# Output projection as 32 column-block tiles, started while the last scan group drains

## The reference, cut to what matters

```python
hx = modulate(rms_norm(x, g0), mx[0], mx[1]);  hc = modulate(rms_norm(ctx, g0), mc[0], mc[1])
z, xs, B, C, dt = split(silu_conv(h @ w_in))          # w_in: 2048 x 10368
y  = D_skip * xs + sum over two directions of ssd_scan(xs, dt, a, B, C, state from ctx)
yx = rms_norm(y * silu(z), norm_g) @ w_out            # w_out: 4096 x 2048
x  = x + mx[2] * yx
h2 = modulate(rms_norm(x, g1), mx[3], mx[4])
out = x + mx[5] * moe(h2)                             # 32 experts, top-1 group, top-2 experts
```

## Time and profile before

| | |
|---|---|
| median of 3 runs | 2303.89 us (2303.46 to 2305.78) |
| the profiled execution | 2307.22 us |
| its span | 2305.7 us |
| PE / PEld / DVE / ACT / POOL busy | 88 / 53 / 44 / 21 / 5 % of the span |
| last projection of the groups ends | about 1020.9 us |
| last matmul of the output projection ends | about 1260.4 us |
| first transposes of h2 | 1282.9 us |
| HBM traffic | 660 MB, mean 286 GB/s |

### The profile page before, as it was taken

One profiled execution on the slowest core, in us unless ns is written; L12 is line 12 of the kernel. 1 busy time (PEld: TensorE's weight loads), 2 busy tenths in 40 slices (PEclk: granted clock), 3 DMA queues, 4 the chain that ended last, 5 costly groups with the idle time before them and its releaser, 6 DMA issues. The chain is left out here.

```text
span 2305.7 us, 28693 instructions
## 1 busy us (share of the span) xinstructions
PE 2033.7 (88%) x10596; PEld 1219.1 (53%) x10596; DVE 1011.0 (44%) x1619; ACT 487.5 (21%) x519; POOL 108.2 (5%) x148
## 2 busy tenths in 40 slices
PE   4789999999999999975998489888888888888888
PEld 2368777777777777754787343333333333323332
DVE  2264656565655555654555632222222222222223
ACT  3132333333424243422443200000000000000000
POOL 0000000000000000002900000000000000000000
PEclk8689999999999999987999599999999999999999
DMA  7967575666665656563555269999999999999997
GB/s 292 380 198 216 179 210 175 198 186 186 186 198 174 205 168 205 178 203 120 221 197 192 100 248 422 422 422 422 422 422 422 422 422 422 422 422 422 422 422 310
DMA packets 296347, 660.37 MB, mean 286 GB/s; under 512 B 15936, under 2 KB 186304, under 8 KB 241904
## 3 DMA queue, kind: packets, MB, share of 16 engines
q1 hardware_dynamic: 288672, 635.27, 74.4%
q0 software_dynamic: 6672, 24.29, 2.8%
q10 hardware_dynamic: 960, 0.23, 0.0%
HBM read 653.28 MB, written 6.46 MB: 286 GB/s over the span
## 5 line engine op out<-in xcount | busy, mean ns | idle before, releaser
L1614 PE MATMUL bank<-wt,xe 128*64 128x512 f32 x2048 | 466.3, 597 | 111.5 <-DMA wt<-in_moe_w_up 108.4
L1395 PE MATMUL bank<-hTh,whi 128*128 128x256 f32 (+1 forms) x1280 | 414.2, 344 | 0.0
L1396 PE MATMUL bank<-hTl,whi 128*128 128x256 f32 (+1 forms) x1280 | 406.1, 337 | 0.0
L1290 DVE TENSOR_TENSOR x<-x,bank 128x512 f32<-128x512 f32 x256 | 158.3, 680 | 544.6 <-PE bank L1601 544.6
L1614 PEld LDWEIGHTS bank<-wt,xe 128*64 128x64 f32 x2048 | 158.3, 137 | 413.6 <-issue 410.2
L1395 PEld LDWEIGHTS bank<-hTh,whi 128*128 128x128 f32 x1280 | 243.8, 190 | 80.2 <-issue 47.5
L1396 PEld LDWEIGHTS bank<-hTl,whi 128*128 128x128 f32 x1280 | 244.1, 191 | 24.1
L893 DVE TENSOR_TENSOR wlo<-raw,whi 128x2048 fp32r<-128x2048 f32 x80 | 183.2, 2290 | 130.8 <-ACT whi L665 130.4
L1400 PE MATMUL bank<-hTh,wlo 128*128 128x256 f32 (+1 forms) x1280 | 234.9, 336 | 0.0
L1639 PE MATMUL bank<-wt,hdn 128*64 128x512 f32 x1024 | 226.8, 595 | 1.4 <-DVE hdn L1302 1.4
L1400 PEld LDWEIGHTS bank<-hTh,wlo 128*128 128x128 f32 x1280 | 199.8, 190 | 24.9
(11 more groups left out here) (286 smaller groups left out, 1814.8 us busy)
## 6 DMA issues: line engine op xcount, KB each, us to landing
wt<-in_moe_w_gate SPq DMA_DIRECT2D x128, 1024.0 KB, 23.4
wt<-in_moe_w_up SPq DMA_DIRECT2D x128, 1024.0 KB, 25.5
wt<-in_moe_w_down SPq DMA_DIRECT2D x128, 1024.0 KB, 22.4
raw<-in_ssm_w_in SPq DMA_DIRECT2D x80, 1024.0 KB, 6.1
raw<-in_ada_w SPq DMA_DIRECT2D x79, 1024.0 KB, 5.2
raw<-in_ssm_w_out SPq DMA_DIRECT2D x32, 1024.0 KB, 4.8
fr<-in_ada_w SPq DMA_DIRECT2D x17, 1024.0 KB, 14.0
bc<-cum_d POOLq DMA_DIRECT2D x32, 512.0 KB, 7.1
```

The source lines that it names most:

```text
L1290: dve.tensor_tensor(x1[:, tt, cols], x1[:, tt, cols], banks[(1, 3, 6, 7)[nb]][:, :], ALU.add).then_inc(s_acc2, 1)
L1395: pe.matmul(bank[:, 0:width], wh[:, k, :], hTh[:, k, 0:width], start=(k == 0), stop=False)
L1396: last = pe.matmul(bank[:, 0:width], wh[:, k, :], hTl[:, k, 0:width], start=False, stop=False)
L1614: last = pe.matmul(banks[0][SLOTS * h:SLOTS * h + SLOTS, :], xe[:, k, :], wt[2 * q + h][:, FF * i:FF * i + FF], start=(k == 0), stop=(k == ...
```

## The change

1. **First stage.** Nine slots instead of seven; only the last two wait for the transposes. The four `fr` slots at 16, 24, 48 and 56 KB lie over the halves of `hTh` and `hTl` that are filled last. B's tile of `w_in` is loaded right behind the dt tile. PE does blocks 0 to 3, then four times: one block, a quarter of dt, a quarter of projection B (`b_part`). C and x0 are projected before `dt_turn`, which writes banks 4 and 5; DVE's and ACT's dt work is mixed with the work for B, C and x0.
2. **Scan output.** `finish` gets two more DVE operations: a copy of y to fp32r and the difference. POOL stores both (`yh_d`, `yl_d`; twice the bytes). They are loaded straight to `yh` and `yl`; `norm_g` goes to `w_out`'s rows instead.
3. **Output projection.** 32 tiles of 512 rows by 512 columns (`OTILES`), seven of column block 0, seven of block 1, the last group's two, then blocks 2 and 3. ACT and DVE work on each in four pieces with `norm_g` as scale. The first ten tiles stand in the drain's ten steps. A column block leaves PSUM two tiles after it is done; the squares' reduction comes two tiles before the end.
4. tanh of B and x chunks is written in place by ACT; the MoE's last two weight buffers, `x1`, `h2` and others lie elsewhere.

```diff
-    FSLOT = [0, 1, 2, 3, 4] * 2 + [5, 6, 0, 1, 2, 3, 4] * 3 + [5, 6]
+    FSLOT = [0, 1, 2, 3, 4, 5, 6] * 2 + [7, 8, 3, 4, 5, 6, 7, 8, 3, 4, 5, 6, 7, 8, 4, 6, 7, 8, 4]
+    OTILES = [(nb, q) for nb in range(2) for q in range(GROUPS - 1)] + [(0, GROUPS - 1), (1, GROUPS - 1)]
+    OTILES += [(nb, q) for nb in range(2, 4) for q in range(GROUPS)]
...
# SP
+                if pos == DT_POS:
+                    front_free(max(q for q in range(FRONT) if FSLOT[q] == 0))
+                    sp.dma_start(w_view(raw, 0), w_in[:, :, bass.ds(w_in_at(0, 0), P)]).then_inc(s_raw[0], 16)
...
+            for i, (nb, q) in enumerate(OTILES):
...
+                    sp.wait_ge(s_lo, M_OUT + i - RAW + 1)
+                sp.dma_start(a_view(raw_of(OUT0 + i)), w_out[:, 4 * q:4 * q + 4, 512 * nb:512 * nb + 512])
+                if i == RAW - 1:
+                    sp.wait_ge(s_win, M_OUT)
+                    for g in range(GROUPS - 1):
+                        y_load(g)
+                if i == OLAST[0] - 1:
+                    y_load(GROUPS - 1)
+                    sp.dma_start(x1[:, :, :], t["x"][0]...)
+                    sp.dma_start(rw...)   ...
# POOL, per k of 32
+                pool.tensor_tensor(yk, yh[:, k, :], yl[:, k, :], ALU.add)
                 pool.tensor_tensor(yk, yk, yk, ALU.mult)
                 pool.tensor_tensor(ysq[:, 1, :], ysq[:, 1, :], ysq[:, 0, :], ALU.add)
# ACT
+            def out_hi(i):
+                act.wait_ge(s_raw[raw_of(OUT0 + i)], ...)
+                act.wait_ge(s_wh, m - 1)
+                act.wait_ge(s_lo, m - 1)
+                for j in range(4):
+                    last = act.activation(whi[:, m % 2, 512 * j:512 * j + 512], raw[...], ACT.Copy, scale=ngcol[:, 4 * q + j:4 * q + j + 1])
...
+                    if not w:
+                        out_hi(n + 1)
                     if ssd and n in (0, 4):
                         decays(s, n // 4)
# DVE
                 dve.tensor_tensor(ybuf[:, c % 2, :], ybuf[:, c % 2, :], zs[:, c, :], ALU.mult).then_inc(s_fin2, 1)
+                dve.wait_ge(s_fin2, GC * s + (c + 1))
+                dve.tensor_copy(yhb[:, c % 2, :], ybuf[:, c % 2, :]).then_inc(s_fin3, 1)
+                dve.wait_ge(s_fin3, GC * s + (c + 1))
+                dve.tensor_tensor(ylb[:, c % 2, :], ybuf[:, c % 2, :], yhb[:, c % 2, :], ALU.subtract).then_inc(s_yout, 1)
...
+            def out_lo(i):
+                dve.wait_ge(s_hi, m + 1)
+                dve.wait_ge(s_win, m - 1)
+                for j in range(4):
+                    last = dve.scalar_tensor_tensor(wlo[...], raw[...], ngcol[...], whi[...], ALU.mult, ALU.subtract)
...
+                    if not w:
+                        out_lo(n + 1)      # ahead of differences, weights, finish of the step
...
+            for i in range(NCH + 1, NOT):
+                out_lo(i)
+                for nb in range(3):
+                    if i == OLAST[nb] + 2:
+                        leave(nb)
+            dve.wait_ge(s_yt, 1)
...         # mean, rstd, then the residual of blocks 0 to 2
+            leave(3)
+            for tt in range(TT):
+                residual(3, tt)
# PE
+            for j in range(4):
+                ada_block(4 + j)
+                ada_turn(4 + j)
+                dt_part(j)
+                b_part(j)
...
+            def out_tile(i):
+                if q == 0:
+                    pe.wait_ge((s_drain, s_a2r, s_stev, s_fin1)[nb], (NCH * GROUPS, 1, GROUPS, IC)[nb])
+                pe.wait_ge(s_yld[q], 32)
+                pe.wait_ge(s_hi, m + 1)
+                for a, ring in ((yh, whi), (yl, whi), (yh, wlo)):
...
+                    for j in range(4):
+                        for tt in range(TT):
+                            last = pe.matmul(banks[2 * nb + tt][:, :], a[:, 4 * q + j, P * tt:P * tt + P], ring[:, m % 2, 512 * j:512 * j + 512], ...)
...
+                    if not w and n == 0:
+                        turn(s, 8)
+                    if not w:
+                        out_tile(n)
...         # then turn 9, states (n = 2), y_chunk (n = 3 and 6) as before
+            for i in range(NCH, NOT):
+                out_tile(i)
+                if i == NOT - 3:
+                    pe.wait_ge(s_yss, IC)
...         # the squares' reduction
```

More of the change, by code:

```diff
@@ L252, in build @@
         s_x = [sem(f"s_xin{i}") for i in range(2)]
-        s_fr = [sem(f"s_fr{i}") for i in range(4)]
+        s_fr = [sem(f"s_fr{i}") for i in range(6)]
         s_const = sem("s_const")
@@ L450, in group_loads @@
                 for pos, (kind, n) in enumerate(LOADS):
+                    if first and pos == 0:
+                        continue
                     slot_free(g, pos, first)
@@ L668, in _, with conv_first @@
             round_rows(0)
+            round_rows(1)
             act.wait_ge(front_sem(DT_POS), 16 * (FNTH[DT_POS] + 1))
             act.activation(whi[:, 0, :], front_tile(DT_POS), ACT.Copy).then_inc(s_hi, 1)
-            for j in range(1, len(BLOCK_PAIRS)):
+            conv_hi(0, 0)
+            for j in range(2, len(BLOCK_PAIRS)):
                 round_rows(j)
-            conv_hi(0, 0)
             conv_hi(0, 1)
+            def conv_first(g, n):
+                width = T if CHUNKS[n][0] in "Bx" else L
+                act.wait_ge(s_win, NCH * g + (n + 2))
+                if not (isinstance(g, int) and g == 0 and n < 2):
+                    act.wait_ge(s_prod, NCH * g + (n - 1))
+                col = conv_col(g, n)
+                act.activation(cv[:, n % 2, 0:width], banks[(n + 1) % 2][:, 0:width], ACT.Identity,
+                               scale=tapc[:, 1, bass.ds(col, 1)], bias=tapc[:, 3, bass.ds(col, 1)]).then_inc(s_cvA, 1)
             act.wait_ge(s_dtx, 1)
@@ L716, in steps @@
                         ada_row(g, n // 9)
[L717 removed]
+                    if w and n + 1 < NCH and not (isinstance(g, int) and g == 0 and n < 2):
                         conv_hi(g, n + 1)
@@ L761, in _ @@
             steps(GROUPS, False, True)
[L764 to L772 removed]
+            for i in range(NCH + 1, NOT):
+                out_hi(i)
             act.wait_ge(s_mean, 2)
@@ L900, in _ @@
             ada_rows(3)
+            modulated(1)
             lo(0, 0, front_tile(DT_POS), free=False)
-            modulated(1)
+            conv_lo(0, 0)
             for j in range(2, len(BLOCK_PAIRS)):
@@ new lines, in residual @@
+            def residual(nb, tt):
+                cols = slice(512 * nb, 512 * nb + 512)
+                dve.scalar_tensor_tensor(x1[:, tt, cols], h2[:, tt, cols], rstd[:, 4 + tt:5 + tt], x1[:, tt, cols],
+                                         ALU.mult, ALU.add).then_inc(s_x1, 1)
+            for i in range(NCH + 1, NOT):
+                out_lo(i)
+                if i == OLAST[0] + 2:
+                    dve.wait_ge(s_modb, 48)
+                for nb in range(3):
+                    if i == OLAST[nb] + 2:
+                        leave(nb)
@@ L1463, in c_times_b @@
                 pe.wait_ge(s_prod, NCH * g + 2)
-                if not (isinstance(g, int) and g == 0):
+                if isinstance(g, int) and g == 0:
+                    pe.wait_ge(s_tokm, 1)
+                else:
                     pe.wait_ge(s_stev, g)
@@ L1488, in ada_columns @@
                 last.then_inc(s_asum, 1)
+            def out_tile(i):
+                nb, q = OTILES[i]
+                m = M_OUT + i
+                if q == 0:
+                    pe.wait_ge((s_drain, s_a2r, s_stev, s_fin1)[nb], (NCH * GROUPS, 1, GROUPS, IC)[nb])
+                if q == 0 and nb == 1:
+                    pe.wait_ge(s_Tev, NTURN * GROUPS)
+                pe.wait_ge(s_yld[q], 32)
+                pe.wait_ge(s_hi, m + 1)
+                for a, ring in ((yh, whi), (yl, whi), (yh, wlo)):
+                    if ring is wlo:
+                        last.then_inc(s_wh, 1)
+                        pe.wait_ge(s_lo, m + 1)
+                    for j in range(4):
+                        for tt in range(TT):
+                            last = pe.matmul(banks[2 * nb + tt][:, :], a[:, 4 * q + j, P * tt:P * tt + P], ring[:, m % 2, 512 * j:512 * j + 512],
+                                             start=(q == 0 and j == 0 and a is yh and ring is whi),
+                                             stop=(q == GROUPS - 1 and j == 3 and ring is wlo))
+                last.then_inc(s_win, 1)
             def steps(g, w, ssd):
```

351 lines of the change are left out of this document (171 added, 180 removed).

## The result

| | before | after |
|---|---|---|
| median of 5 runs each, us | 2305.78 (2303.46 to 2308.48) | 2291.99 (2287.15 to 2296.88) |
| ratio | | 0.9936, interval 0.9923 to 0.9949 |
| profiled execution, us (span) | 2307.2 (2305.7) | 2294.2 (2292.2) |
| first DVE packs of group 0 | 187.6 | 179.6 |
| last DVE packs of the groups | 1023.2 | 1036.0 |

The change won 13.8 us, where 31 were forecast. From h2's transposes on both kernels take 1022.8 us, as the prediction's first paragraph had it. Ahead of them the two traces differ by 13.5 us: first stage -8.0, from the first packs to T +20.8, output projection -20.2, tail -6.1. (A minus sign means faster.)

A forecast was written before the change was run, and what follows sets the result against it. Each stage has its own limit: DMA and a serial chain first, PE in groups and output projection, serial DVE/ACT tail, DMA-chained MoE. 2307.2 - 16 + 11 - 19.5 - 6 = 2276.7, less 3.3: 2273 us; range 2257 to 2293.

The forecast's parts named there:

- the prediction's first paragraph: MoE: lasts as long as before once h2 is ready; only microseconds won ahead of h2's transposes come out at the end.
- Groups: Scan groups: two new DVE operations per chunk lengthen PE's wait for L1109; loss 11 us, bounds 14 and 0.
- First stage: Start to projection z0: DMA hole closes and dt's chain ends earlier; gain 16 us, bounds 8 and 22.
- The last tile comes at 113.5: First stage: last `ada_w` tile about 4.5 us earlier, with loads of the last four tiles held up about 4 us.
- z0 starts at 154: End of first stage: after dt's transposes PE starts projection z0 at about 154 us, instead of 170.
- Drain and output projection: After the last projection: tiles run inside the drain, last matmul at T+220; gain 19.5 us, bounds 28 and 8.
- Tail: Last matmul to h2's first operation: fewer gate operations and residuals left, 7.3 instead of 13.2 us; gain 6, bounds 4 and 8.
- Rival 1: Groups: the new DVE operations are hidden since DVE is idle half the time; 2262 us, chance 0.12.
- Rival 2: Output projection: POOL's squares are late, an operation taking more than 1.28 us beside DVE; taken at 2284 us, chance 0.17.
- Rival 3: Drain: raw ring's three slots serialise tiles, last chunks at T+115 instead of T+79; 2309 us, slower than before, chance 0.04.
- one of the signs that I had given against myself: Drain: the prediction is wrong if `w_out` loads are what ACT waits for there.
- Rival 4: Drain: tiles run cold, PE's bursts between waits at the lower clock, at most 10 us on the path; 2283 us, chance 0.12.

The follow-up runs named there:

- The last experiment: Against the changed kernel with parts and packs behind differences, B behind blocks, router weights last: z0, C and B work moved inside first group's dt chain; 2248.15 us.

## Why the prediction was half right

*The mechanisms.* All four stages moved the way the sum had it, and the result lies at the range's upper edge, but the predicted time was 19 us too low, and 13.8 us were won where 31 were forecast. Of the 17 us that the four terms were off, the groups make 9.8, the first stage 8.0. Term by term:

- **Groups, +11 forecast, +21 measured.** This is the step that failed most. Its mechanism holds: the new DVE operations stand in the chain to packs, the period has grown, and taking them out brings everything back. The wait grew by 12.4 us where I had 11. The sum put at nothing that a longer pause is paid twice, the second time in clock, 8.4 us over the groups; so the loss lies outside the bounds of 0 and 14, and the last projection ended at 1033.7 instead of about 1016. I had the earlier trace rows with nearly full clock in the groups beside a pause of 1.85 us, and took it for granted that 3.4 us would leave it so; I weighed the rule on bursts for the drain alone.
- **First stage, -16 forecast, -8 measured**, the lower bound. "The last tile comes at 113.5" failed: PE finished the last block at 118.7, since B's quarters stood between its blocks and held the slots. I had priced held slots at 4 us and named them, with the lower clock, as the lower bound's condition; the slots were held although the clock over the last two blocks was 0.91 to 1.00. Without B there the last tile is used at 112.9 to 115.9 in three executions. (The sum's range also errs: 16 with bounds of 8 and 22 moves the time 8 up but only 6 down.) Then "z0 starts at 154": PE turned dt at 154.1 and drained z0 at 164.2, where the forecast had about 160. And I ended the walk there, while the raw slot that z0's low part frees late cost PE another 3.5 us. The last experiment takes both of those waits away.
- **Drain and output projection, -19.5 forecast, -20.2 measured.** Last y chunk at T + 74 (79), last matmul at T + 219.3 (220). The pause before tile 14 was 6.8 us (I had about 4); moving the router's weights takes it away. It was paid twice as well, with 1.7 us of clock. The last y chunk came 5 us early and the squares cost nothing, which covered both: that the term came out so near is in part luck.
- **Tail, -6 forecast, -6.1 measured**: 7 us from the last matmul to h2.

*The rivals.* Rival 1 (hidden, 2262) is refuted by two runs: the operations cost 21 to 23 us where they stand. Rival 2 (squares late) did not occur: POOL was done at T + 177 and then idle for 42.5 us; an operation took 0.83 to 0.95 us on average, under the 1.23 of before; the loss did not grow with the number of DVE's pieces. Rival 3 did not occur, though one of the signs that I had given against myself did: in the drain ACT waited once for a `w_out` load, 9.1 us for tile 3, whose load SP issued at 1050.1 behind the y of seven groups. PE was not held by it; it was waiting for `xtok` until 1065.3, did `states` first, and had tile 3 ready behind that. Rival 4 (cold tiles) was right about the clock and wrong about the place: the drain kept its forecast, and the groups lost.

What decides whether the clock falls behind a given pause is open: pauses of the same length in the same place are sometimes followed by it and sometimes not, and no run varied the work behind the pause.

## What to carry to other kernels

When work is added to an in-order engine, ask in which chain it stands and not how busy the engine is; moving four small operations a group behind the work that others wait for was worth more (22.7 us) than the whole change (13.8). Price a lengthened pause of PE twice, by the wait and by the clock behind it. And after a gain is booked, follow the rings one turn further: a slot freed late by one engine's order (here behind the dt chain) gives part of it back.

## What the runs showed that I had not expected

- A pause of 1.85 us in the matmuls costs its length and, in one case of seven, 1.5 us of clock; one of 2.53 us costs the 1.5 us in six cases of seven; one of 3.62 us hardly more than that (8.5 us over six intervals against 7.3). The cost comes in steps of about 1.5 us, now and then 2.5.
- One load of 128 x 16 rows of 32 floats held SP's queue for 10.46 us (L506) ahead of the next tiles of `w_out`. The time is not the load's own: the same load held the queue for 2.72 us in the kernel before and for 3.97 in the run with the router last. In the changed kernel it stood directly behind a load of y and 2 MB of `x`, and that `x` load itself held the queue for 4.31. What sets it was not tested. Moving the router's loads won 8.1 us.
- DVE's pieces of 128x512 took 0.73 us at the least and up to 1.28; from 1115 to 1211 us, beside POOL's squares, 1.11 on average. At four pieces a tile that is 4.4 us of a period of 5.45, and it did not bind. By the rule that the prediction drew on (the Trainium skill, "SBUF — State Buffer", Who interferes with whom) the two exclude each other; the trace agrees in that both took longer together (POOL's first operation of a k up to 1.23 us against 0.72 at the least). That four pieces lose up to four times what one operation lost did not come out.
